# A two-layer hybrid encoder: the token dimension taken in halves where stages meet, the residual through PSUM

## The reference, cut to what matters

```python
def rms_norm(x, g):
    y = x * rsqrt(mean(x * x, axis=-1, keepdims=True) + EPS)
    return y * g

for l in range(DEPTH):                        # DEPTH = 2
    h = rms_norm(x, ln_pre_mix[l])
    m = hybrid_mixer(h, w_in[l], ...)         # ends with merged @ w_out
    x = x + rms_norm(m, ln_post_mix[l])
    h = rms_norm(x, ln_pre_ffn[l])
    gu = h @ ffn_w_gu[l]
    f = (silu(gu[..., :D_FF]) * gu[..., D_FF:]) @ ffn_w_down[l]
    x = x + rms_norm(f, ln_post_ffn[l])
return x
```

## Time and profile before

| | before |
|---|---|
| median of 3 runs | 1851.4 us (1851.23 to 1851.89) |
| profiled execution | 1853.21 us |
| its span, first to last instruction | 1851.4 us |
| mean granted TensorE clock | 0.971 of full |
| TensorE matmul busy | 1719.6 us (93%) |
| VectorE busy | 921.1 us (50%) |
| ScalarE busy | 406.1 us (22%) |
| GpSimd busy | 1131.7 us (61%) |
| chain that ended last | TensorE 78%, VectorE 16%, issue 3%, ScalarE 2%, GpSimd 1% |
| DMA | 151.34 MB, mean 82 GB/s |

### The profile page before, as it was taken

One profiled execution on the slowest core, in us unless ns is written; L12 is line 12 of the kernel. 1 busy time (PEld: TensorE's weight loads), 2 busy tenths in 40 slices (PEclk: granted clock), 3 DMA queues, 4 the chain that ended last, 5 costly groups with the idle time before them and its releaser, 6 DMA issues.

```text
span 1851.4 us, 21177 instructions
## 1 busy us (share of the span) xinstructions
PE 1719.6 (93%) x8162; PEld 1404.2 (76%) x8162; DVE 921.1 (50%) x1621; ACT 406.1 (22%) x875; POOL 1131.7 (61%) x1172
## 2 busy tenths in 40 slices
PE   7999999899879999999879999998999699999996
PEld 6778678677667888888677787786776588888885
DVE  5755754865555333410277557558654644343102
ACT  3440313223231111100134313023332211111000
POOL 6536456343666887877584373653446668887773
PEclk9999999999989999999889999999999899999998
DMA  5112222111111222222231131121112122222221
GB/s 221 69 46 87 73 82 78 69 46 69 68 68 69 91 91 102 89 91 97 76 123 69 46 114 69 69 89 48 69 46 70 67 73 109 92 91 93 94 94 61
DMA packets 26035, 151.34 MB, mean 82 GB/s; under 512 B 3211, under 2 KB 4491, under 8 KB 12080
## 3 DMA queue, kind: packets, MB, share of 16 engines
q1 hardware_dynamic: 22176, 141.21, 21.2%
q10 hardware_dynamic: 3760, 8.78, 1.5%
HBM read 147.88 MB, written 4.70 MB: 82 GB/s over the span
## 4 chain that ended last, share of the span: by engine, by line
PE 78%; DVE 16%; issue 3%; ACT 2%; POOL 1%; DMA 0%; ACTq 0%; DVEq 0%
PE main L636 11%; PE main L533 11%; PE main L534 11%; PE main L535 11%; PE work L533 8%; PE work L534 8%; PE work L535 8%; PE turn L693 2%; PE pv L533 2%; DVE prob L1445 2%; PE pv L535 1%; PE pv L534 1%; DVE yt L1516 1%; DVE pt_lo L1229 1%; DVE tiny L1257 1%
## 5 line engine op out<-in xcount | busy, mean ns | idle before, releaser
L475 POOL TENSOR_SCALAR w_hi<-raw 128x512 fp32r<-128x512 f32 (+3 forms) x576 | 381.4, 671 | 662.5 <-issue 642.2
L479 POOL TENSOR_TENSOR w_lo<-raw,w_hi 128x512 fp32r<-128x512 f32 (+3 forms) x576 | 748.8, 1310 | 0.0
L636 PE MATMUL main<-h_hi,w_lo 128*128 128x512 f32 x512 | 208.7, 408 | 0.0
L636 PE MATMUL main<-h_hi,w_hi 128*128 128x512 f32 x512 | 208.3, 407 | 0.0
L533 PE MATMUL main<-h_hi,w_hi 128*128 128x512 f32 x480 | 192.3, 401 | 16.6 <-DVE h_lo L1231 16.0
L636 PE MATMUL main<-h_lo,w_hi 128*128 128x512 f32 x512 | 207.4, 405 | 0.0
L535 PE MATMUL main<-h_hi,w_lo 128*128 128x512 f32 x480 | 189.7, 395 | 0.0
L534 PE MATMUL main<-h_lo,w_hi 128*128 128x512 f32 x480 | 189.7, 395 | 0.0
L533 PE MATMUL work<-h_hi,w_hi 128*128 128x512 f32 x480 | 188.6, 393 | 0.0
L534 PE MATMUL work<-h_lo,w_hi 128*128 128x512 f32 x480 | 188.2, 392 | 0.0
L535 PE MATMUL work<-h_hi,w_lo 128*128 128x512 f32 x480 | 187.9, 391 | 0.0
(11 more groups left out here) (233 smaller groups left out, 3009.0 us busy)
## 6 DMA issues: line engine op xcount, KB each, us to landing
raw<-stream SPq DMA_DIRECT2D x106, 1024.0 KB, 4.8
raw<-stream SPq DMA_DIRECT2D x32, 704.0 KB, 4.1
...
```

The lines of the kernel that those rows point to most:

```text
L475: pool.tensor_scalar(w_hi[:, slot, parts[q]], raw[:, slot, parts[q]], 1.0, 0.0, ALU.mult, ALU.add).then_inc(piece_hi, 1)
L479: e = pool.tensor_tensor(w_lo[:, slot, part], raw[:, slot, part], w_hi[:, slot, part].bitcast(F32), ALU.subtract)
L636: mm = pe.matmul(main[m % 2][:, :], w, (h_lo if which == 1 else h_hi)[:, k, :], start=(s % STEPS == 0), stop=(s % STEPS == STEPS - 1))
```

## The change

`HALVES` are tokens 0 to 255 and 256 to 511. The changes go together:

- **w_out**: tiles 0 to 3 stay whole; tiles 4 to 7 are made for half 0 first, then for half 1 (`OUT_TILES`). Statistics and spread of half 0 stand among the matmuls of half 1.
- **Residual**: VectorE writes factor times kept tile into a PSUM bank and adds `x` to it there; ScalarE copies the sum to `x` and makes `h_hi` and the square; VectorE makes `h_lo` from the bank. Half 0 comes before half 1. GpSimd has no part in it but for the last output. Two banks are used in turn.
- **Gate/up**: the first piece does half 0 with statistics and spread of half 1 of the norm before in it, then the second piece half 0, then both half 1. The two pairs of banks change places.
- **Down**: the last tile is made in halves, with statistics and spread of half 0 among the matmuls of half 1.
- **Latent projection**: half 0 (two token tiles) over all 8 feature tiles, then half 1. In the second layer the statistics of half 1 of the output norm stand after feature tile 1 of half 0, their spread between the halves. Six gate matmuls now stand ahead of the statistics.
- **Sums of squares** of the two input norms move to GpSimd (`input_sum`), 14 adds of 128x256 each, in its list behind the two latent pieces and behind the second gate/up piece.
- **Last output**: VectorE scales, GpSimd adds all 8 tiles of half 0 and tiles 5 to 7 of half 1, VectorE adds tiles 0 to 4 of half 1; 16 stores.
- The gains of the input norm get a small tile of their own (`gain_in`), and the load of the other parameters stands behind the second weight piece.

The core of the diff; functions that are replaced as a whole are shown in the new form, with the common indentation taken off:

```diff
 WOUT0 = len(MAIN)
-GUM0 = WOUT0 + KD
+HALVES = (slice(0, S // 2), slice(S // 2, S))
+OUT_TILES = [(d, slice(0, S)) for d in range(KD // 2)] + [(d, half) for half in HALVES for d in range(KD // 2, KD)]
+DOWN_TILES = [(d, slice(0, S)) for d in range(KD - 1)] + [(KD - 1, half) for half in HALVES]
+GUM0 = WOUT0 + len(OUT_TILES)
 DOWNM0 = GUM0 + 2 * KF
-N_MAIN = DOWNM0 + KD
+N_MAIN = DOWNM0 + len(DOWN_TILES)
...
 BRANCH_STEPS = KD * STEPS
-GATE_BEFORE = dict(D=[24, 48, 48, 78, 80, 83, 85, 88, 90, 93, 95, 98], A=[0], B=[0], C=[0])
...
         pv = psum("pv")
-        ffn_bank = [main, work[:2]]
+        ffn_bank = [work[:2], main]
+        x_bank = [work[2], pv]
...
+def input_sum(l, name):
+    for half, cols in enumerate(HALVES):
+        first = at(l, N_IN_SUM, (KD - 1) * (2 * (name == "pre_ffn") + half))
+        sq, total = norm_f["sq"], norm_f["sum"][:, cols]
+        for d in range(1, KD):
+            pool.wait_ge(in_squared, at(l, 4 * KD, IN0[name] + KD * half + d + 1))
+            if d > 1:
+                pool.wait_ge(in_sum, first + d - 1)
+            pool.tensor_tensor(total, sq[:, 0, cols] if d == 1 else total, sq[:, d, cols], ALU.add).then_inc(in_sum, 1)
 for l in range(0, L):
-    split(l, 0, 0, PIECES[0][1], (main_done, at(l, N_MAIN, 1)))
-    for n in range(1, GU0 + 2):
-        split(l, n, n % 2, PIECES[n][1], free_after(l, n - 2) if n >= 2 else (main_done, at(l, N_MAIN, 1)))
-
-    for d in range(MIX_DVE, KD):
-        pool.wait_ge(scaled, at(l, 2 * KD, d + 1))
-        pool.tensor_tensor(x[:, d, :], x[:, d, :], kept_m[:, d, :], ALU.add).then_inc(x_pool, 1)
+    split(l, 0, 0, PIECES[0][1], (down_half, l * KD) if l else (main_done, 1))
+    split(l, 1, 1, PIECES[1][1], (main_done, at(l, N_MAIN, 1)))
+    input_sum(l, "pre_mix")
+    for n in range(2, GU0 + 2):
+        split(l, n, n % 2, PIECES[n][1], free_after(l, n - 2))
+    input_sum(l, "pre_ffn")
...
+    for half in range(2):
+        if l and half:
+            spread(l - 1, "post_ffn", 1)
+            pe.wait_ge(kept_done, l * N_KEPT)
+        for k in range(KD):
+            if half == 0 and k % 4 == 0:
+                wait_piece(l, PIECE[f"Dlat{k // 4}"])
+            wait_split(l, ("h", "pre_mix", half, k))
+            a, slot = N_LAT * (k % 4), k // 4
+            for t in (2 * half, 2 * half + 1):
+                mm = three(lat_bank[t][:, 0:N_LAT],
+                           h_hi[:, k, P * t:P * t + P], h_lo[:, k, P * t:P * t + P],
+                           w_hi[:, slot, a:a + N_LAT], w_lo[:, slot, a:a + N_LAT], k == 0, k == KD - 1)
+                if k == KD - 1:
+                    mm.then_inc(pv_done if t == 1 else work_done, 1)
+            if half == 1 and k == 3:
+                mm.then_inc(lat_half, 1)
+            if l and half == 0 and k == 1:
+                mean_square(l - 1, "post_ffn", 1)
+    gate_steps(l, "D", 0)
     pe.wait_ge(loaded, 16)
+    input_square(l, "pre_mix")
+    gate_steps(l, "D", 1)
     spread(l, "pre_mix")
...
+    def out_tile(m, ks=range(KD)):
+        d, cols = OUT_TILES[m]
+        n = PIECE[f"out{d // 2}"]
+        if ks[0] == 0:
+            wait_piece(l, n)
+            if m < 2:
+                pe.wait_ge(y_used, at(l, 4 * KD, 3 * KD + 6 + m + 1))
+            else:
+                pe.wait_ge(kept_done, l * N_KEPT + m - 1)
         for k in ks:
+            if m == 0:
+                wait_split(l, ("merged", k))
+            a = 256 * k + P * (d % 2)
+            mm = three(main[m % 2][:, cols], w_hi[:, n % 2, a:a + P], w_lo[:, n % 2, a:a + P],
+                       h_hi[:, k, cols], h_lo[:, k, cols], k == 0, k == KD - 1)
+        if ks[-1] == KD - 1:
+            mm.then_inc(main_done, 1)
+    for m in range(KD):
+        out_tile(m)
+    out_tile(KD, range(3))
+    mean_square(l, "post_mix", 0)
+    out_tile(KD, range(3, KD))
+    out_tile(KD + 1, range(2))
+    spread(l, "post_mix", 0)
+    out_tile(KD + 1, range(2, KD))
+    out_tile(KD + 2)
+    out_tile(KD + 3)
...
+    def gate_up(i, s, js, ks=range(KD), cols=slice(0, S)):
+        for k in ks:
             for j in js:
                 a = 256 * k + P * j
+                mm = three(ffn_bank[s][j][:, cols], w_hi[:, s, a:a + P], w_lo[:, s, a:a + P],
+                           h_hi[:, k, cols], h_lo[:, k, cols], k == 0, k == KD - 1)
+                if k == KD - 1 and cols.stop == S:
                     mm.then_inc(main_done, 1)
+    def first_gate_up(half, k):
+        wait_split(l, ("h", "pre_ffn", half, k))
+        gate_up(0, 0, (0, 1), range(k, k + 1), HALVES[half])
     wait_piece(l, GU0)
+    for k in range(KD):
+        first_gate_up(0, k)
+        if k == 1:
+            mean_square(l, "post_mix", 1)
+        if k == 6:
+            spread(l, "post_mix", 1)
     wait_piece(l, GU0 + 1)
+    pe.wait_ge(kept_done, l * N_KEPT + len(OUT_TILES))
+    gate_up(0, 1, (0, 1), cols=HALVES[0])
+    for k in range(KD):
+        first_gate_up(1, k)
+    gate_up(0, 1, (0,), range(4), HALVES[1])
+    input_square(l, "pre_ffn")
+    gate_up(0, 1, (0,), range(4, KD), HALVES[1])
+    gate_up(0, 1, (1,), range(4), HALVES[1])
     spread(l, "pre_ffn")
+    gate_up(0, 1, (1,), range(4, KD), HALVES[1])
     for i in range(1, KF // 2):
         for s in range(2):
             pe.wait_ge(piece_split, l * NP_ + 2 * i + (GU0 + s + 3))
+            for j in range(2):
+                pe.wait_ge(ffn_up if j else ffn_scaled, l * KF + 2 * i + s + 1)
...
+    def down_part(m, s, ks=range(KH)):
+        d, cols = DOWN_TILES[m]
+        if m < KD:
+            wait_piece(l, PIECE[f"down{d}{s}"])
+        for k in ks:
+            kk = KH * s + k
+            if m == 0:
+                wait_split(l, ("act", kk))
+            mm = three(work[m % 2][:, cols], w_hi[:, s, P * k:P * k + P], w_lo[:, s, P * k:P * k + P],
+                       act_hi[:, kk, cols], act_lo[:, kk, cols], kk == 0, kk == KF - 1)
+        if ks[-1] == KH - 1 and (s or m != KD - 1):
+            mm.then_inc(main_done if s else down_half, 1)
+    for m in range(len(DOWN_TILES)):
+        if m < 2:
+            pe.wait_ge(ffn_up if m else ffn_scaled, at(l, KF, KF + 1))
+        else:
+            pe.wait_ge(kept_done, l * N_KEPT + len(OUT_TILES) + m - 1)
+        if m < KD:
+            down_part(m, 0)
+        else:
+            down_part(m, 0, range(4))
+            mean_square(l, "post_ffn", 0)
+            down_part(m, 0, range(4, KH))
+            spread(l, "post_ffn", 0)
+        down_part(m, 1)
+    if l == L - 1:
+        mean_square(l, "post_ffn", 1)
...
+def keep(l, name, m):
+    sc, kept = scratch_of[name], kept_of[name]
+    d, cols = (OUT_TILES if name == "post_mix" else DOWN_TILES)[m]
+    bank = (main if name == "post_mix" else work)[m % 2]
+    act.wait_ge(main_done, at(l, N_MAIN, (WOUT0 if name == "post_mix" else DOWNM0) + m + 2))
+    if m >= 2:
+        if (name, m - 2) in SUMMED_AT:
+            act.wait_ge(summed, at(l, len(SUMMED), SUMMED_AT[(name, m - 2)] + 1))
         else:
+            act.wait_ge(turn_done, at(l, N_TURN, TURN_AT[("stat", name, 0)] + 1))
...
+def next_input(l, name, half, d, done, banks):
+    n, cols = done + KD * half + d + 1, HALVES[half]
+    act.wait_ge(x_done, n)
+    act.activation(x[:, d, cols], banks[d % 2][:, cols], ACT.Copy).then_inc(x_kept, 1)
+    act.wait_ge(x_kept, n)
+    norm_input(l, name, half, d)
...
         act.wait_ge(merged_done, at(l, 3 * KD, 2 * KD + d + 1))
         hi(l, ("merged", d), h_hi[:, d, :], merged[:, d, :], 0.5)
+    for m in range(KD + 2):
+        keep(l, "post_mix", m)
+    for half in range(2):
+        for d in range(KD):
+            next_input(l, "pre_ffn", half, d, at(l, 4 * KD, 0), x_bank)
+            if half == 0 and d in (2, 5):
+                keep(l, "post_mix", KD + 2 + d // 3)
     for i in range(0, KF // 2):
         for s in range(2):
             act.wait_ge(ffn_scaled, l * KF + 2 * i + s + 3)
...
+def residual(l, name, half, then, banks):
+    to, cols, kept = "pre_ffn" if then == l else "pre_mix", HALVES[half], kept_of[name]
+    first = at(l, 4 * KD, 2 * KD * (name == "post_ffn") + KD * half)
+    def low(d):
+        gain = gain_in[:, then, d:d + 1] if to == "pre_mix" else param(to, d)
+        lo(then, ("h", to, half, d), h_lo[:, d, cols], banks[d % 2][:, cols], h_hi[:, d, cols], gain)
+    dve.wait_ge(kept_done, l * N_KEPT + KEPT0[name] + (KD if half == 0 else len(OUT_TILES if name == "post_mix" else DOWN_TILES)))
     for d in range(KD):
+        bank = banks[d % 2][:, cols]
+        if d >= 2:
+            dve.wait_ge(x_kept, first + d - 1)
+            dve.wait_ge(lo_done, at(then, N_SPLIT, SPLIT_AT[("h", to, half, d - 2)] + 1))
+        dve.tensor_tensor(bank, kept[:, d, cols], factor(l, name, half), ALU.mult).then_inc(scaled, 1)
+        dve.wait_ge(scaled, first + d + 1)
+        dve.tensor_tensor(bank, x[:, d, cols], bank, ALU.add).then_inc(x_done, 1)
+        if d:
+            low(d - 1)
+        if half == 0 and name == "post_mix" and d in (0, 2, 4):
```

(28 more changed lines are left out.)

355 lines of the change are left out of this document (143 added, 212 removed).

## The result

The changed kernel takes 1871.9 us (median of four runs, 1871.0 to 1872.6); the kernel before, run beside it, 1851.6. The ratio is 1.0103, 95% interval 1.0092 to 1.0115: 1.0% slower. The forecast was 1850.7, the range ended at 1859. The profiled execution has a span of 1870.8 us.

The account below looks back on a forecast made before the run. TensorE, busy 1719.6 of 1851.4 us, was taken to bound the kernel. Head +6, w_out to gate/up -2 x 2.5, down to next latents +0.5 and tail -2.2 summed to -0.7: 1850.7 us, range 1842 to 1859.

Parts of the forecast that it names:

- meeting 2: Down projection to the next layer's latent projection, once: net +0.5 us, bounds -4 to +4.
- meetings 1: w_out to gate/up, once a layer: 45.2 against 47.7 us, a gain of 2.5 each, bounds gain 6.5 to loss 2.
- the tail: End of the program after the last matmuls: 17.5 against 19.7 us, -2.2 (0 to -4).
- the head: Program start to the transposes of the latents: +6 us, bounds +3.5 to +8.
- the cut down tile: Last down tile: cutting adds 0.9 us, statistics and spread 1.45, together 2.35.
- the low clock: Matmuls at the 1.2 GHz level after TensorE waits: one such stretch costs 1.6 to 1.9 us.
- The signs named for the waits: TensorE waits several us before first gate matmuls, released by GpSimd's w_lo; three short waits between w_out and gate/up.
- rival 2: Slower by GpSimd's queue, first gate piece behind the second half in both layers: 1863 us, mild form 1857; chance 0.28.
- (b): w_out: last weight piece not split in time, a wait of 2.1 us, perhaps a slow stretch, 0.9 on average.
- The second root: Down to next latents: VectorE stops after tile 4 for it, beside the other split, 5.3 to 9.3 us.
- root less disturbed -2: Head: the root meets less disturbance, taking 2 us off the +8.1 of later statistics.
- (d): w_out to gate/up: second root starts after half 0's residual (6.0 us), beside a split, until 10.6; spread to 11.6.

Follow-up runs that it names:

- experiment 5: Changed kernel with the residual kept in SBUF, not put through PSUM, and without ScalarE's copy back: 1879.3 us, ratio 1.0147.
- Experiment 4: Changed kernel with each weight piece of the cut last down tile used for both halves before the next piece: 1865.0 us, ratio 1.0073.
- Experiments 1 and 2: 1: changed kernel, sums of squares ahead of the latents on VectorE, not GpSimd, 1860.0 us; 2: changed kernel, latents' statistics ahead of gate matmuls, 1865.0 us.
- all edits up to 9: Changed kernel with the first four experiments' edits, head halves undone, tail's second root first, first half's input sums back on GpSimd: 1847.9 us, ratio 0.9973.
- experiment 3: Changed kernel with only the last two w_out tiles cut into halves, not four: 1864.6 us, ratio 1.0073.
- experiment 12: Kernel with all edits up to 9, plus matmuls ahead of both spreads between w_out and gate/up, and GpSimd's split waiting for the root: 1841.3 us, ratio 0.9937.

## Why the prediction was wrong

The forecast was -0.7 us, the spans differ by +19.4. The 20.1 us between them are 7.1 in meeting 2, 4.6 in the two meetings 1, 2.8 in the tail, 2.7 in the head and 2.9 elsewhere. Two steps of the prediction failed: the cut down tile, put at 2.35 us with no wait for its second weight piece, and the low clock, counted in meeting 1 and for six gate matmuls and at nothing in the other places.

**Right.** The signs named for the waits: several us ahead of the first gate matmul in both layers, released by GpSimd; gates in the head at 39.3 (39.38), though by two errors that cancel, since the sums there began at 19.7 us and not 21.2 and took 12.3 and not 10.5; the two waits on weights in meeting 1 (2.1 each; 2.64 and 2.04); additions through PSUM undisturbed (428 ns), whose price had no row of its own and was taken from PSUM reads, with experiment 5 as the proof; the rival that won was rival 2, slower by GpSimd's queue, though past its end of 1863 and with its condition met only in part: it asked for over 8 us a split and over 0.8 an addition, and the runs show 8.2 for the split of the last w_out piece and 0.88 for an addition in the head, but 7.3 and 0.74 at meeting 2, where most was lost.

**Meeting 2, +7.6 for +0.5, is the largest miss.** (i) The step "The last down tile is cut and carries statistics and spread: 2.35" left out that this tile uses up its first weight piece too fast for the split of the second: a wait of 2.16. The prediction has this step for w_out, under (b), and not for down. Experiment 4 took that wait away, and meeting 2 gave 5.0 us. (ii) The second root was put at 5.3 us, as if the second half's statistics were ready; they stand in TensorE's queue behind two latent tiles that themselves wait for a weight (930.65), so the root ran from 935.8 to 940.6. (iii) A tile of a half takes 1.37 us and not 1.25, since the low part with its PSUM operand takes 0.48, where the earlier trace rows had 0.42 for another form, and the next multiply starts 0.57 behind its start, for which I had 0.35. So the second half's first low was used 5.3 us later than forecast, and the rest of the queue moved with it; the split itself took 7.3, as said. (iv) The first 13 gate matmuls behind the wait and the statistics between them ran at 1.2 GHz, and so did most matmuls from 931.95 to 945.3. Counted over the whole stretch, the waits are 15.8 us before and 15.6 after, and slow matmuls cost about 1.3 and 8.3: (i) to (iii) say where TensorE stood still, but nearly all of the 7.6 us is matmuls that ran at the lower level.

**Head, +8.7 for +6.** The gates came as forecast. The missing 2.7 are the low clock behind a wait of 5.8 us (statistics end 1.2 later than forecast) and the term "root less disturbed -2", of which 0.6 came: the root is no longer what the transposes wait for, 42 gate matmuls behind the statistics are. Experiments 1 and 2 show both halves of the mechanism: an earlier weight gave 5.4, earlier statistics 2.7, and with all edits up to 9 it takes 47.9, close to the 47.5 of the kernel before.

**Meeting 1, +0.7 and -1.1 for -2.5 each.** The end of w_out comes 7.1 later, forecast 5.8: the wait is 0.5 longer, and the slow stretch behind it that had been counted at half came in full. The second spread starts 13.2 after that, forecast 10.6: 1.0 of it is eight tiles at 0.12 more, 1.1 a root of 5.7 us for 4.6. From there to the second pair 28.1 us pass for the forecast 28.8. The step at fault is (d), the second root: it was to start 6.0 us behind the end of w_out and to end at 10.6, and it started at 7.4 and ended at 13.1. The two waits on weights were in the sum, with 2.1 each and 0.9 for a slow stretch, and experiment 3 shows about what they were put at: without them meeting 1 is 4.1 and 4.5 us shorter. In layer 1 the same waits stand behind 1.7 us less, by the clock.

**Tail, +0.6 for -2.2.** Again the second piece of the cut down tile: 2.16 of waiting and 1.5 of low clock behind it, the second by chance: experiment 3 has the wait without it, and its tail takes 34.0. From the last statistics on, the forecast of 15.1 stands against 14.2.

**Elsewhere, +2.9 for 0.** The mixers and the large matmul stages run the same matmuls; layer 1's mixers took 2.0 longer. The runs show such differences of 1 to 3 us in stretches whose program was not changed, always with another share of matmuls at 1.2 GHz: meeting 2 went from 76.3 to 79.3 in experiment 3. The term was not in the sum and belongs in the range. What decides in a given run where the low clock falls is open.

How often matmuls run at low clock was the weight that was missing in the rivals. Counted from the timelines, with the difference of the two paces for each wide matmul at the slower one (0.20 us for 512 columns), low clock cost about 22 us in all in the kernel before, 42 in the changed one, and 22 in experiment 12. TensorE's waits in the four kinds of place sum to about 67 us before and 69 after, over the whole span to 120 and 115: what changed is how they are cut up and what the clock did behind them. The mean granted clock doesn't show it, 0.971 before and 0.969 after, because it counts idle time too. In the kernel before much of the low clock fell into the long wait, as in this window with no matmul in it:

```profile
921.00:924.00 3.00, 0.00 (x0) 0.00 (x0) 2.97 (x5) 0.05 (x1) 3.00 (x3) 0.50 0.00 0
```

This is a count and no experiment: only the tail of experiment 3 has the same waits with another clock, and that by chance. The Trainium skill, "TensorE: Matmul & The Clock Gate", § HAM oscillation, warns that gaps between groups of matmuls bring the clock down each time. The trace agrees for the waits of 5.79 and 6.23 us and not for every wait of 2 to 3 us (see the last section). The prediction cited it and priced only a part of the places.
